# Prompt attention's scores as three products of rounded parts, gated output parked in device memory, seven page slots

## The reference

```python
def mla_prompt_attention(q_nope, q_rope, c_kv, k_rope, w_uk, w_uv):
    ...
    k_nope = jnp.einsum('btl,lhn->bthn', c_kv, w_uk)
    v = jnp.einsum('btl,lhv->bthv', c_kv, w_uv)
    scale = (MLA_NOPE + MLA_ROPE) ** -0.5
    ...
        s = (jnp.einsum('bqhn,bkhn->bhqk', qn, k_nope)
             + jnp.einsum('bqhr,bkr->bhqk', qr, k_rope)).astype(jnp.float32) * scale
        s = jnp.where(key_pos[None, :] <= q_pos[:, None], s, -jnp.inf)
        p = jax.nn.softmax(s, axis=-1).astype(v.dtype)
        return jnp.einsum('bhqk,bkhv->bqhv', p, v)

def trunk_layer(x, start, mla_attend, s0, conv_prefix, mem_k, mem_v, p):
    ...
    o_mla = mla_attend(q_nope, q_rope, c_kv, k_rope).reshape(B, T, MLA_WIDTH)
    o_hg, s_new = hgrn2_group(z[..., OFF_HG:], p['lb'], p['norm_hg'], s0)
    x = x + jnp.einsum('btc,cd->btd', jnp.concatenate([o_mla, o_hg], axis=-1), p['w_out'])
    x = x + memory_attention(rms_norm(x, p['norm_memx']), mem_k, mem_v, p['w_mq'], p['w_mo'])
    y, conv_tail = conv_ffn(rms_norm(x, p['norm_ffn']), ...)
    x = x + y
```

## Time and profile before

| | us |
|---|---|
| median of 3 runs | 1842.02 |
| lowest, highest | 1838.22, 1850.56 |
| the profiled execution | 1832.29 |
| its span | 1830.3 |
| busy in it: PE, PEld | 1760.6, 1587.0 |
| busy in it: DVE, ACT, POOL | 1216.3, 529.8, 576.6 |

### The profile page before, as it was taken

The page is one execution under the profiler, slowest core; times in us unless marked ns, Lnnn a source line. Parts: engine busy times, 40 slices in busy tenths (PEclk is TensorE's granted clock), DMA queues, the critical chain, the costliest instruction groups (busy, mean ns, idle before and its releaser), DMA issues.

```text
span 1830.3 us, 31679 instructions
## 1 busy us (share of the span) xinstructions
PE 1760.6 (96%) x13502; PEld 1587.0 (87%) x13502; DVE 1216.3 (66%) x1550; ACT 529.8 (29%) x948; POOL 576.6 (32%) x415
## 2 busy tenths in 40 slices
PE   6999999998999999899987999999999999999998
PEld 6999999985665555599976899999999999999998
DVE  5587887676778999844419458862773474574575
ACT  5233321544554444421205321110110010010026
POOL 2222222240000555323255233333333333333630
PEclk9999999999999999999999999999999999999999
DMA  7221221240211999521236111111111111111202
GB/s 248 54 60 36 60 60 47 45 146 28 98 60 68 397 409 411 219 75 32 81 117 229 36 58 47 38 44 58 47 34 56 50 35 48 57 41 47 76 23 96
DMA packets 162569, 177.08 MB, mean 97 GB/s; under 512 B 21998, under 2 KB 146948, under 8 KB 158044
## 3 DMA queue, kind: packets, MB, share of 16 engines
q1 hardware_dynamic: 146512, 94.07, 17.3%
q0 software_dynamic: 7168, 75.50, 10.3%
q10 hardware_dynamic: 8750, 5.49, 1.0%
HBM read 161.86 MB, written 13.27 MB: 96 GB/s over the span
## 4 chain that ended last, share of the span: by engine, by line
PE 81%; DVE 14%; issue 1%; ACT 1%; DMA 1%; POOL 0%; SPq 0%; ACTq 0%; DVEq 0%; POOLq 0%
PE PS L833 22%; PE PS L835 22%; PE PS L834 22%; DVE KPT L2330 5%; PE PS L870 3%; PE PS L1050 2%; DVE KPT L2335 2%; PE PS L1089 1%; PE PS L915 1%; DVE KRT L2321 1%; DVE dsm L2340 1%; DVE Pm L2464 1%; PE PS L1358 1%; PE PS L1360 1%; PE PS L1359 1%
## 5 line engine op out<-in xcount | busy, mean ns | idle before, releaser
L765 POOL CAST whi<-wraw 128x1024 fp32r<-128x1024 f32 (+4 forms) x142 | 139.5, 982 | 891.1 <-PE PS L835 838.8
L833 PE MATMUL PS<-BH,whi 128*128 128x344 f32 x1152 | 368.9, 320 | 0.0
L834 PE MATMUL PS<-BL,whi 128*128 128x344 f32 x1152 | 367.1, 319 | 0.0
L835 PE MATMUL PS<-BH,wlo 128*128 128x344 f32 x1152 | 367.0, 319 | 0.0
L767 POOL TENSOR_TENSOR wlo<-wraw,whi 128x1024 fp32r<-128x1024 f32 (+4 forms) x142 | 312.7, 2202 | 11.4
L834 PEld LDWEIGHTS PS<-BL,whi 128*128 128x128 f32 x1152 | 216.2, 188 | 0.5 <-issue 0.5
L833 PEld LDWEIGHTS PS<-BH,whi 128*128 128x128 f32 x1152 | 216.2, 188 | 0.5 <-issue 0.5
L835 PEld LDWEIGHTS PS<-BH,wlo 128*128 128x128 f32 x1152 | 216.2, 188 | 0.0
L833 PE MATMUL PS<-XH,whi 128*128 128x344 f32 x528 | 176.9, 335 | 3.4 <-DVE XL L1935 3.4
L2419 DVE TENSOR_TENSOR XT<-PS,XT 128x1032 f32<-128x1032 f32 x48 | 59.1, 1232 | 174.4 <-PE PS L835 174.3
L834 PE MATMUL PS<-XL,whi 128*128 128x344 f32 x528 | 169.3, 321 | 0.0
(11 more groups left out here) (459 smaller groups left out, 3652.2 us busy)
## 6 DMA issues: line engine op xcount, KB each, us to landing
wraw<-in_w_up_dram SPq DMA_DIRECT2D x44, 512.0 KB, 3.7
wraw<-in_w_in_dram SPq DMA_DIRECT2D x20, 512.0 KB, 4.1
wraw<-in_w_down_dram SPq DMA_DIRECT2D x24, 256.0 KB, 2.6
wraw<-in_w_down_dram SPq DMA_DIRECT2D x16, 320.0 KB, 3.2
xt_kept<-XT SPq DMA_DIRECT2D x1, 4128.0 KB, 12.8
XT<-xt_kept SPq DMA_DIRECT2D x1, 4128.0 KB, 14.7
xstage<-in_x_prompt_dram SPq DMA_DIRECT2D x8, 512.0 KB, 10.4
wraw<-in_w_out_dram SPq DMA_DIRECT2D x8, 512.0 KB, 4.2
```

Of the source, the lines that this page charges most:

```text
L765: gp.tensor_copy(hi, raw).then_inc(w_hi_done, 1)
L833: pe.matmul(out, wh[:, t, 0:m], hi[:, tile(t), s], start=(t == first), stop=False)
L834: pe.matmul(out, wh[:, t, 0:m], low, start=False, stop=False)
L835: ins = pe.matmul(out, wl[:, t, 0:m], hi[:, tile(t), s], start=False, stop=(t == last))
```

## The change

1. **Scores.** `QHs`, two buffers of 4 x 1024 columns, take the rounded parts of one pair's two queries and two keys; `QLo` lies in place over `QK4` and takes the remainders. A score is now three products with fp32r operands: high by high, high by low, low by high.
2. **Who makes the parts.** For pair 0, ACT makes the rounded parts directly behind the last rotary copies (`pair_high(0, n)`), and DVE makes the four remainders ahead of the copies of value blocks 0 to 3. For pairs 1 to 3, ACT makes one part at the end of each of steps 4 to 7 of the pair before, and POOL subtracts (`pair_low`).
3. **HGO.** The buffers `QHs` lie over `HGO` and over the weight buffers. `HGO` (2.1 MB) is written to device memory (`gated_kept`) during the query projections and read back when group 25 is done and the rotary rows of all groups are transposed.
4. **Slots.** There are 7 slots, placed elsewhere: slot 0 in the space of `XT`, slots 1 to 3 in that of pairs 0 to 2, slot 4 in that of `HGO`, slot 5 in the space of the weight buffers, slot 6 in that of the values. The output weights may be loaded when group 26 is done (`FREE`), and POOL may split them when all rotary rows are transposed. The turned weights `PTs` of the samples have one buffer instead of two.
5. **Seam.** ACT makes `cat_high` 0 to 3 in one go; the parts lie in one tensor `CAT`.

```diff
-SLOTS = 6
+SLOTS = 7
+SLOT_OF = [g % SLOTS for g in range(GT)]
...
-        rc0, rk0, rk2, rk3, rk4 = place(W0, S0, *page(0), *[page(n)[1] for n in (2, 3, 4)])
+        rc5, rk1, rk2, rk3, rk4 = place(W0, S0, page(5)[0], *[page(n)[1] for n in (1, 2, 3, 4)])
...
+        rc1, = place(A0, A0 + PAIR, page(1)[0])
+        rc2, sel32 = place(A0 + PAIR, A0 + 2 * PAIR, page(2)[0], ("sel32", [P, 32], F32))
+        rc3, = place(A0 + 2 * PAIR, A0 + 3 * PAIR, page(3)[0])
+        rc4, = place(B0, R1, page(4)[0])
...
+        QHs = [at(f"QH{n}", [P, 4, T], F32R, a) for n, a in enumerate((B0, W0))]
+        QLo = at("QLo", [P, H // 2, 4, TT], F32R, A0)
...
+        FREE = GT - SLOTS + 1
...
             if j in (job_no[("out", 0)], job_no[("out", 1)]):
-                full(sp, ("go", GT - 2))
+                full(sp, ("go", FREE))
...
+                if j == job_no[("un", 0)]:
+                    emptied(sp, ("sot", HG - 1))
+                    sp.dma_start(gated_kept, HGO[:, :, :].rearrange("p h t -> p (h t)")).then_inc(hgo_out, 16)
                 if j == job_no[("out", 1)]:
+                    full(sp, ("go", GT - SLOTS))
+                    sp.wait_ge(hgo_out, 16)
+                    sp.wait_ge(kr_turned, GT)
+                    sp.dma_start(HGO[:, :, :].rearrange("p h t -> p (h t)"), gated_kept).then_inc(hgo_back, 16)
+                    full(sp, ("go", GT - 2))
                     sp.dma_start(wuv[:, :, :], cols(w_uv, 0, H * VD)).then_inc(wuv_in, 16)
-                    full(sp, ("go", GT - 1))
...
+            def pair_low(p2):
+                for n in range(4):
+                    gp.wait_ge(qk_hi, 4 * p2 + n + 1)
+                    gp.tensor_tensor(QLo[0:QK, p2, n, 0:T], QK4[0:QK, p2, n, 0:T], QHs[p2 % 2][0:QK, n, :], ALU.subtract).then_inc(qk_lo, 1)
...
-                        if g == 1:
+                        if g == 0:
                             emptied(gp, "qlat")
...
+                        if g < 3:
+                            pair_low(g + 1)
...
+                    gp.wait_ge(kr_turned, GT)
...
-                        ins = pe.matmul(out, q_of(h)[0:QK, q * P:q * P + P], k_of(h)[0:QK, c0:c1], start=True, stop=True)
+                        mine = slice(q * P, q * P + P)
+                        pe.matmul(out, hi[0:QK, m, mine], hi[0:QK, 2 + m, c0:c1], start=True, stop=False)
+                        pe.matmul(out, hi[0:QK, m, mine], lo[0:QK, 2 + m, c0:c1], start=False, stop=False)
+                        ins = pe.matmul(out, lo[0:QK, m, mine], hi[0:QK, 2 + m, c0:c1], start=False, stop=True)
...
+            def pair_high(p2, n):
+                if (p2, n) == (0, 0):
+                    act.wait_ge(hgo_out, 16)
+                    act.wait_ge(krk_new, 1)
+                elif (p2, n) == (1, 0):
+                    full(act, ("uk", H // 2 - 1))
+                elif n == 0:
+                    full(act, ("S", pair_end[p2 - 2]))
+                act.activation(QHs[p2 % 2][0:QK, n, :], QK4[0:QK, p2, n, 0:T], ACT.Copy).then_inc(qk_hi, 1)
+
+            for n in range(4):
+                pair_high(0, n)
...
+                if n % 12 in (4, 5, 6, 7) and n < 36:
+                    pair_high(n // 12 + 1, n % 12 - 4)
...
-                if g >= 2:
-                    full(act, ("go", g - 2))
+                if g:
+                    full(act, ("go", g - 1))
...
-            cat_high(0), cat_high(1)
+            act.wait_ge(hgo_back, 16)
+            for n in range(4):
+                cat_high(n)
...
             for n in range(NT):
+                if n < 4:
+                    ve.wait_ge(qk_hi, n + 1)
+                    ve.tensor_tensor(QLo[0:QK, 0, n, 0:T], QK4[0:QK, 0, n, 0:T], QHs[0][0:QK, n, :], ALU.subtract).then_inc(qk_first, 1)
                 full(ve, ("v", n))
...
-            full(ve, ("go", GT - 2))
+            ve.wait_ge(hgo_back, 16)
             cat_low(0), cat_low(1)
```

More of the change, by code:

```diff
@@ L184, in build_program @@
         Ps = place(S0, S0 + 4128, *[(f"Ps{n}", [P, 512], F32) for n in range(2)])
-        PTs = place(S0 + 2 * 4128, S0 + 3 * 4128, *[(f"PTs{n}", [P, 4, P], F32) for n in range(2)])
+        PTs, rk6 = place(S0 + 2 * 4128, S0 + 3 * 4128, ("PTs", [P, 4, P], F32), page(6)[1])
+        rc, rk = [rc0, rc1, rc2, rc3, rc4, rc5, rc6], [rk0, rk1, rk2, rk3, rk4, rk5, rk6]
         dsm = at("dsm", [P, TT], F32, S0 + 4128)
@@ L1244, in _ @@
             for c in range(2, KD):
-                dense(("out", c), CHi, CLo, lambda t: pe.wait_ge(cat_lo, order.index(t) + 1), order=order)
+                dense(("out", c), CAT, CLo, lambda t: pe.wait_ge(cat_lo, order.index(t) + 1), order=order, tile=high_at)
             def memory_turns(h, t):
```

74 lines of the change are left out of this document (44 added, 30 removed).

## The result

| | before | changed |
|---|---|---|
| median, us | 1842.38 (17 runs, 1838.22 to 1852.3) | 1851.19 (17 runs, 1842.36 to 1854.35) |
| ratio, 95% interval | | 1.0039 [1.0027, 1.0052] |
| the profiled execution, its span | 1832.29, 1830.3 | 1846.02, 1844.2 |

The forecast was 1841; the time lies inside its range, but the change moved the kernel up where no movement was forecast, and it came close to the figure of the second rival, 1851.5.

What follows compares the result with a forecast made beforehand. No engine was taken to be full in prompt attention, DVE to bound the samples' attention, and waits the seam. 8.4 - 7.2 + 4.5 - 6.7 = -1.0 us against 1832.29, put on the median: 1841 us, range 1830 to 1859.

Steps and rivals of the forecast that it cites:

- the second rival: In attention, the port decides: POOL's subtractions delay DVE's scaling; with 15 us the sum is +9.5, 1851.5; chance 0.20.
- Value stage, +8.4: Value stage: blocks follow DVE's 2.6 us, scores start later, +7.4 us, plus 1.0 for the lower clock; bounds +6.1 and +10.8.
- Scores, -7.2: Prompt attention: three fp32r products shorten a pair's scores by 2.8 us, 1.8 taken as gain; bounds 0 and -11.
- the rule that it names beside it: Scores: a weight load costs its columns over 1.2 GHz, 107 ns for 128; the pair would save 2.3, not 2.8.
- Parts for pairs 1 to 3, +4.5: Prompt attention: POOL's subtractions delay DVE's scaling at the port, 1.5 us for each of three pairs; bounds 0 and 12.
- the walk over four steps: Attention, pair 2: four steps followed with POOL's subtraction over DVE's scaling; 1.3 us a pair, taken as 1.5.
- The clock in attention, put at nothing: Attention: the sum had no term for the clock; its 1.0 us for the clock lay in the value stage.
- a rival at 0.08: Attention: TensorE idles more, lower-clock stretches come back; six more of 3.4 us cost 10, giving 1851; chance 0.08.
- HGO's trip and the single PTs, 0: HGO's write and read-back are covered, with 4 us to spare; TensorE's order makes one PTs buffer free; 0.
- The slots, 0: Samples' attention: DVE bounds the stage, so a seventh slot gives nothing and pages come in time; 0.
- Seam, -6.7: Seam: earlier output weights remove a 4.7 us wait and 2.0 us of slow products; bounds -8 and -3.3.
- what would show it: Signs: 6 us gap, scores 7 to 11 later, 0.23 apart, pairs 34 to 36, scaling above 1, output products within 1.

Runs made afterwards that it cites:

- e2: The changed kernel with scores as one product with f32 operands and no rounded parts or remainders; 1836.37 us, ratio 0.9967 to the kernel before.
- e3: The changed kernel with f32 scores for pair 0 alone, pairs 1 to 3 keeping three products; 1842.28 us, ratio 0.9999 to the kernel before.
- e7: The changed kernel with pair 0's four remainders made by DVE behind value blocks 4 to 7; 1841.6 us, ratio 1.0025 to the kernel before.
- e10: e2 with the parts of pairs 1 to 3 made by ACT and POOL, read by no product; 1844.06 us, ratio 1.0009 to the kernel before.
- e14: e10 without POOL's twelve subtractions, ACT still making its rounded parts; 1838.92 us, ratio 0.998 to the kernel before.
- e1: The changed kernel with the samples' pages rotated through six slots, the seventh taking page 28 alone; 1858.03 us, ratio 1.0087 to the kernel before.
- e4: The kernel before with one buffer for the samples' turned weights PTs; 1840.48 us, ratio 0.9998 to the kernel before.
- e8: The changed kernel with the twelve remainders of pairs 1 to 3 made by DVE instead of POOL; 1845.26 us, ratio 1.0024 to the kernel before.
- e12: The kernel before, unchanged, run once more for a second profile; 1849.36 us in its one execution.
- e9: The changed kernel without the gathers of groups 7 to 31, all engine instructions kept; 1835.65 us, ratio 0.997 to the kernel before.
- e6: e2 with TensorE multiplying the samples' values one group later; 1871.14 us, ratio 1.0173 to the kernel before.
- e13: e2 with ACT copying the last group's values right behind cat_high 0 and 1 at the seam; 1834.95 us, ratio 0.997 to the kernel before.

## Why the prediction was wrong, step by step

By ratios, the change splits into -6.1 us (e2: seam, slots, HGO), +7.4 (from e3 to the changed kernel: pair 0) and +5.9 (from e2 to e3: pairs 1 to 3), in sum +7.2. The prediction had -6.7, +6.6 (8.4 - 1.8) and -0.9 (4.5 - 5.4). The three are differences of ratios with intervals of 2 to 4 us each, so here is the first half by traces too. Against e2's profile the changed kernel has +7.8 us in the value stage, +6.5 in pair 0, +0.4, +0.6 and -1.5 in pairs 1 to 3, in sum +13.8 (13.3 by the ratios). The prediction had +8.4, -0.3 (-1.8 + 1.5), -0.3, -0.3 and -1.8, in sum +5.7. **Of the 8.1 us that it missed, 6.8 lie in pair 0.** Two of its steps are wrong there: the price of the parts, and a clock that the sum left at its level of before.

- **Value stage, +8.4: right,** in mechanism and size. +7.8 in the two profiles; the first scores come at 421.1 to 423.1 in the four profiles with this order, at 412.0 to 415.3 in the others with f32 scores in pair 0. e7 shows the wait that makes it.
- **Scores, -7.2: the size a little high.** The undisturbed pair 3 gives 1.5 us, not 1.8. That the products are 0.23 apart was right; but the first of a score costs 0.34, 0.11 more in most of a pair's 12 units, and that is up to 1.3 of the 2.8 us by which the prediction had a pair's products shorten. Products of 128 keys start 0.06 and 0.11 us apart (549.50, 549.56 and 549.67), between its 0.067 for all and the 0.107 of the rule that it names beside it.
- **Parts for pairs 1 to 3, +4.5: the first step that failed.** The mechanism (port) was the right one, and e10 against e14 shows it alone; its size was not. Two sizes entered: POOL's 1.90 us was 2.35 to 2.5, and the walk over four steps was made in pair 2 and used for pair 0, where DVE also copies the samples' queries, which the walk didn't have (4.4 us of waiting in the changed kernel): +4.5 there in e10, 2.9 in e3. With +1.9 and +2.1 for the others it is 7 to 8.5 us, the upper value with some 1.8 us of half clock in it. The second rival said that the whole turns slower from 5.5 us on, and it did.
- **The clock in attention, put at nothing: the second step that failed.** The sum had 1.0 us for the clock, in the value stage; for attention there was a rival at 0.08 ("more idle time, and stretches at the lower level come back"). Pair 0 with three products had 17 to 23 us of half clock in four profiles of five (10.7 in e1), with f32 scores 3 to 7 (e2 to e4, e10 to e14). The changed kernel has 14.2 us more of it than e2 (17.3 against 3.1), which would cost 7.1 us if TensorE had work all through. Pair 0's 6.5 us more are this clock and the port, less the shorter scores. An estimate, if they simply add up: 2.7 to 2.9 for the port (e10 without its half clock, and e3) and -1.5 for the scores leave some 5.2 us for the clock. No run parts them. Neither the gap (e7) nor the port (e8) is needed for this half clock; that shorter products leave TensorE idle more often, as the rival has it, fits e3 but was not tested alone. Where single stretches of it fell into pairs 1 and 2 (e3), each cost 1.6 us.
- **HGO's trip and the single PTs, 0: right** (e2, e4). **The slots, 0: right for the wrong reason.** "DVE bounds that stage" was read from the profile shown; in 12 of the 13 profiles with gathers and the values in their old place TensorE's chain does, and e1, with six, has the same rhythm. The 11.8 us between the two profiles are between two executions, not two kernels. I put the 10 us between profile and median down to scatter; the stage that held them could have been asked for.
- **Seam, -6.7: half right.** The weights' wait went, but the step "TensorE's next need is then `CLo` 0" was wrong: the bank with the last values was, and ACT frees it behind its parts. 3.1 to 3.3 us came in the changed kernel, 4.3 to 4.5 in e2. The -6.1 of e2 holds something more, most likely in the memory attention (below), which no step had.

**Of what would show it:** the gap of 6 us, the later scores, 0.23 us and the mean of the scaling came as written, the last in pairs 1 and 2 (in pair 0 it is 0.87; pair 3 as before). Pairs of 34 to 36 us did not (36.6 and 37.0), nor output products within 1 us of the last group, nor the period of 5.8 us. On the last "nothing above rests but zero" held.

## What to carry to other kernels

Where no engine is full, a saving is worth only what the chain of waits lets through: score products shorter by at most 2.8 us a pair gave 1.5 us where nothing disturbed them. Operands that GpSimd makes are paid for by VectorE at the port. List every SBUF-to-SBUF operation that VectorE has in the steps where they fall, small ones too (a scaling went from 0.69 to 2.53 us, a copy of 64 columns from 0.18 to 2.37), and walk each stage by itself. If a change leaves TensorE waiting more often, look how much of the stretch has the lower clock, instead of keeping the level of before. If the profiled execution lies outside all timed runs, take a second profile before you call a stage bound by an engine; a copy that frees a bank can be the wait when all operands are there.

## What the runs showed of the hardware

**While pages are gathered, TensorE's chain is slower.** TensorE's scores of a group reach the engines that wait for them then up to 1.1 us later. In the shown profile of before, ACT's copy of the pieces starts 0.49 us behind the first record of the last score products, in all but one group:

```profile
661.85 0.42 PE L1155 MATMUL PS<-KPT,QD 128*32 128x128 f32 x8
```

```profile
662.34 0.60 ACT L1662 ACTIVATE pieces<-PS 128x512 f32<-128x512 f32 x1 [0.28 <-PE PS L1155]
```

In e12 it takes 1.62 us from the one to the other, with both records as long as before, and 0.85 to 1.63 us in 25 groups:

```profile
656.50 0.43 PE L1155 MATMUL PS<-KPT,QD 128*32 128x128 f32 x8
```

```profile
658.12 0.60 ACT L1662 ACTIVATE pieces<-PS 128x512 f32<-128x512 f32 x1 [1.83 <-PE PS L870]
```

Without the gathers (e9) it never happens, and the last groups, with no page left, are back at 5.75 us in every profile but e1's. e9 does not part the landing from POOL's issuing. The landing is the likelier: in the changed kernel the group whose copy starts at 764.39 is still 0.83 us behind, 5 us after the last gather was issued (758.97), with the DMA engines busy for 0.87 of the time; its score records are longer too (0.80 us). Why one execution of the kernel before had the pages at 402 GB/s and was not slowed stays open, and so does where in TensorE or in the memory the time goes.

**The same port in the memory attention.** POOL's eight products of the samples there meet DVE's scaling of the probabilities, which has two sources in SBUF. In the kernel before, the stage's score products ran over 46.2 us and POOL's products were in pieces; in the changed kernel 37.6 us, and in one run:

```profile
970.61 7.89 POOL L792 TENSOR_TENSOR sK<-sK,QB 128x1024 f32<-128x1024 f32 x3 [18.74 <-DMA QB<-q_kept]
981.10 2.34 POOL L792 TENSOR_TENSOR sK<-sK,QB 128x1024 f32<-128x1024 f32 x1 [2.60 <-DMA sK<-in_cache_mem_k_dram]
983.94 2.36 POOL L792 TENSOR_TENSOR sK<-sK,QB 128x1024 f32<-128x1024 f32 x1 [0.49 <-DMA sK<-in_cache_mem_k_dram]
```

```profile
991.76 16.68 POOL L820 TENSOR_TENSOR sK<-sK,QB 128x1024 f32<-128x1024 f32 x6 [18.10 <-DMA QB<-q_kept]
```

DVE's scalings (14 of them; busy us and mean ns) in e6, where the stage took 46.3 us, and in e13, where it took 37.6:

```profile
L2512 DVE TENSOR_TENSOR Pm<-Pm,small 128x512 f32<-128x512 f32 x14 | 18.6, 1327 | 0.5
```

```profile
L2511 DVE TENSOR_TENSOR Pm<-Pm,small 128x512 f32<-128x512 f32 x14 | 10.1, 725 | 0.5
```

The kernel before has 18.4 us and the changed one 10.1: that is the row of -8.6. Of 16 profiles, the 8 in which POOL began at least 11.9 us behind the stage's first score product took 37.5 to 39.1 us, the 8 in which it began 11.4 to 11.7 us behind it 39.7 to 47.1. Kernels with the new seam are in the first group in 7 cases of 12, those with the old one in 1 of 4: that may be the rest of e2's 6.1 us. It is a count of profiles; no run moved POOL's start alone.
